# Trainium2: two transformer blocks on one core, with the products at stage boundaries ordered by row block and some operands produced turned

## What is computed

```python
for i in range(4):                      # first block; kinds A, B, C, A
    q, k, v, ... = split(x @ w_in)      # 12 heads of 64, rotary on the first 16 columns
    mix = attention_of_kind(q, k, v)    # A: indexer picks 64 keys; B: dilated; C: causal here
    mk, mv = split(layer_norm(mem) @ w_mem_kv[i])
    mo = memory_attention(qm, mk, mv)   # 4 heads over 256 memory rows
    x = layer_norm(ALPHA * x + concat(mix, mo) @ w_out[i], ln1)
    x = layer_norm(ALPHA * x + (silu(g) * u) @ w_down, ln2)   # g, u = split(x @ w_gate_up)
for layer in range(2):                  # second block
    h = rms_norm(x, norm_g) * (1 + scale) + shift   # shift, scale, gate from c @ w_ada
    rq, rk, rv, rg, sq, sk, sv, sg = split(h @ w_in_2)         # 8 parts of 512 columns
    y = concat(retention(rq, rk, rv) * silu(rg), stick_breaking(sq, sk, sv) * silu(sg))
    x = x + gate * (y @ w_out_2)
return rms_norm(x, final_g)
```

## Time and profile before

| | |
|---|---|
| median of 3 runs | 1818.16 us (1815.0 to 1821.46) |
| the profiled execution's own time | 1820.88 us |
| its span in the profile | 1819.0 us |
| PE busy / DVE busy / ACT busy | 1670.5 us (92%) / 1090.0 (60%) / 743.6 (41%) |
| mean granted clock of PE | 0.955 |
| moved over DMA | 296.32 MB, mean 163 GB/s |

### The profile page before, as it was taken

The page is one execution under the profiler, slowest core; times in us unless marked ns, Lnnn a source line. Parts: engine busy times, 40 slices in busy tenths (PEclk is TensorE's granted clock), DMA queues, the critical chain, the costliest instruction groups (busy, mean ns, idle before and its releaser), DMA issues.

```text
span 1819.0 us, 19290 instructions
## 1 busy us (share of the span) xinstructions
PE 1670.5 (92%) x7900; PEld 1348.3 (74%) x7900; DVE 1090.0 (60%) x1470; ACT 743.6 (41%) x879; POOL 45.7 (3%) x74
## 2 busy tenths in 40 slices
PE   6888899999988999998899999888999979899987
PEld 5666778878767888786688878666788858776866
DVE  4854566557566566664666557836555667456634
ACT  4434344334433334344343333443343434654372
POOL 1000000000000000000000000000000000000000
PEclk8998899999999999999899999979999989998999
DMA  8341266655324565551266555313456535233421
GB/s 299 135 139 47 93 223 221 227 200 217 116 79 153 210 242 219 208 185 47 94 230 231 208 208 208 127 59 119 168 209 236 214 110 183 107 114 126 170 88 46
DMA packets 43111, 296.32 MB, mean 163 GB/s; under 512 B 4996, under 2 KB 5124, under 8 KB 8976
## 3 DMA queue, kind: packets, MB, share of 16 engines
q1 hardware_dynamic: 38592, 279.99, 42.1%
q0 software_dynamic: 4000, 14.00, 2.4%
q10 hardware_dynamic: 432, 1.11, 0.2%
HBM read 294.03 MB, written 1.05 MB: 162 GB/s over the span
## 4 chain that ended last, share of the span: by engine, by line
PE 79%; DVE 11%; ACT 6%; issue 2%; DMA 1%; POOLq 0%; SPq 0%; DVEq 0%; ACTq 0%; POOL 0%
PE psum L605 22%; PE psum L607 22%; PE psum L606 22%; DVE w_low L1077 3%; PE psum L628 2%; PE psum L787 2%; ACT w_high L898 2%; PE psum L665 2%; ACT work L971 1%; PE psum L799 1%; PE psum L769 1%; DVE neg_max L1333 1%; PE psum L718 1%; DMA w_raw<-in_weights 1%; PE psum L860 1%
## 5 line engine op out<-in xcount | busy, mean ns | idle before, releaser
L1077 DVE TENSOR_TENSOR w_low<-w_raw,w_high 128x2048 fp32r<-128x2048 f32 x242 | 552.1, 2290 | 378.8 <-ACT w_high L898 378.5
L605 PE MATMUL psum<-w_high,xt_high 128*128 128x512 f32 (+1 forms) x1536 | 618.5, 403 | 16.6 <-DVE w_low L1077 8.6
L607 PE MATMUL psum<-w_high,xt_low 128*128 128x512 f32 (+1 forms) x1536 | 606.1, 395 | 0.0
L606 PE MATMUL psum<-w_low,xt_high 128*128 128x512 f32 (+1 forms) x1536 | 605.3, 394 | 0.0
L898 ACT ACTIVATE w_high<-w_raw 128x2048 fp32r<-128x2048 f32 x242 | 459.9, 1911 | 254.6 <-PE psum L607 248.7
L605 PEld LDWEIGHTS psum<-w_high,xt_high 128*128 128x128 f32 x1536 | 296.4, 193 | 80.6 <-issue 13.6
L607 PEld LDWEIGHTS psum<-w_high,xt_low 128*128 128x128 f32 x1536 | 295.3, 192 | 62.7
L606 PEld LDWEIGHTS psum<-w_low,xt_high 128*128 128x128 f32 x1536 | 296.4, 193 | 57.1
L605 PE MATMUL psum<-w_high,ht_high 128*128 128x512 f32 x352 | 138.2, 393 | 6.3 <-DVE ht_low L1383 6.3
L607 PE MATMUL psum<-w_high,ht_low 128*128 128x512 f32 x352 | 137.8, 391 | 0.0
L606 PE MATMUL psum<-w_low,ht_high 128*128 128x512 f32 x352 | 137.7, 391 | 0.0
(11 more groups left out here) (201 smaller groups left out, 1382.0 us busy)
## 6 DMA issues: line engine op xcount, KB each, us to landing
w_raw<-in_weights SPq DMA_DIRECT2D x266, 1024.0 KB, 4.8
norm_params<-in_ln_g POOLq DMA_DIRECT2D x8, 512.0 KB, 4.0
norm_params<-in_ln_b POOLq DMA_DIRECT2D x8, 512.0 KB, 5.3
x_rows<-in_x SPq DMA_DIRECT2D x2, 512.0 KB, 4.6
arena<-in_mem POOLq DMA_DIRECT2D x2, 512.0 KB, 19.7
norm_params<-in_norm_g POOLq DMA_DIRECT2D x2, 512.0 KB, 3.8
out_rows<-x_rows ACTq DMA_DIRECT2D x2, 512.0 KB, 2.6
mem_kv<-in_decay POOLq DMA_DIRECT2D x1, 768.0 KB, 4.8
```

The costliest lines, as they stand in the source:

```text
L605: e.matmul(dst, a_hi, b_hi, start=first, stop=False)
L606: e.matmul(dst, a_hi, b_lo, start=False, stop=False)
L607: return e.matmul(dst, a_lo, b_hi, start=False, stop=last)
L1077: e.tensor_tensor(K.w_lo[:, s, :], K.w_raw[:, r, :], K.w_hi[:, s, :].bitcast(F32), ALU.subtract).then_inc(K.taken.hit(t), 1)
```

## The change

- **Split in two.** `high` and `low` of a tile are steps of their own. After each product step the list has: `low` of the tile rounded last, then `high` of the next if a ring slot is free (`split`). The rings hold five tiles. One background step follows every product step instead of every second.
- **Order at boundaries.** `group` holds all tiles of two blocks (4), multiplies all of them for row block 0 and then all for row block 1. It is used for `w_out`, the first two up steps, the first projections, 7 and 3, and `w_out_2`; the last four down steps are ordered likewise. Sum, norm, rms and modulation of a row block follow its own last product, and the transposes of row block 0 stand among the products of row block 1 (and the other way round).
- **Turned operands.** For sq, sk, memory keys and memory queries the operands change places, so that the product comes out turned: 576 matmuls of 512 columns become 1152 of 256 columns, and 64 transposes of 128 x 128 go (16 + 16 + 32).
- **Memory products** of all four layers are made in layer 0 beside the indexer; those of layers 1 to 3 are put in DRAM (3 transfers out on POOL's queue) and fetched when needed (3 in). They no longer stand at ln2.
- **Feed-forward:** silu and product double buffered, `ht` fourfold; down lags by three steps; one ada tile in each of the steps 3 to 8.
- **Second block:** projections 0 and 1, then sq and sk turned, then 6 and 2 beside stick breaking, then 7 and 3 beside retention, then `w_out_2`.
- Small: one set of norm parameters; sums of ada tiles go through the ring of turning banks; the narrow tile is loaded only as far as it is used (576 columns).

```diff
-RING = 3
+RING = 5
...
+    def split(self):
+        self.low()
+        if self.owed:
+            self.owed -= 1
+            self.high()
+        self.owed, self.given_back = self.owed + self.given_back, 0
...
+    def on(self):
+        self.split()
+        self.step_background()
...
+    def block(self, name, layer, cols, gen, then, what="half"):
+        uses = [self.gemms.take() for _ in range(RB)]
+        for half in range(2):
+            t = self.tile(name, layer, cols, what, 4 * half)
+            for rb in range(RB):
+                self.gemm(t, rb, half, gen, "gemm", uses[rb])
+                if half:
+                    then(rb, uses[rb], t)
+                self.on()
...
+    def group(self, blocks, gen, after):
+        t = [[self.tile(name, layer, cols, what, 4 * half) for name, layer, cols, what, _ in blocks]
+             for half in range(2)]
         for rb in range(RB):
+            uses = [self.gemms.take() for _ in blocks]
+            for half in range(2):
+                for n, (*_, then) in enumerate(blocks):
+                    self.gemm(t[half][n], rb, half, gen, "gemm", uses[n])
+                    if half:
+                        then(rb, uses[n], t[half][n])
+                    after[rb][len(blocks) * half + n]()
...
-    def residual_norm(self, key, left, fill, gen):
...
+    def norm(self, key, rb):
+        self.add("stats", (key, rb))
+        self.add("gain", (key, rb))
+        self.add("bias", (key, rb))
...
+        def rest():
+            self.on()
             self.drain()
+            self.xt(mix, 1)
+            self.norm(key, 0)
...
+        def turned():
+            self.xt(("ff", layer), 0)
+            self.split()
+        self.group([("w_out", layer, h * BLK, "half", sums(h)) for h in range(2)], mix,
+                   [[self.on, self.on, self.on, rest], [self.split, self.split, turned, self.split]])
...
+                    if j.kind in BOTH:
+                        for n in range(2):
+                            dst, c = psum[:, bank, n * SEQ:n * SEQ + SEQ], at + rb * SEQ
+                            cols = slice(c + n * P, c + n * P + P) if turned else slice(c, c + SEQ)
+                            rows = slice(None) if turned else slice(n * P, n * P + P)
...
+                            m = products(e, dst, *both, first and n == 0, last and n == 1)
```

More of the change, by code:

```diff
@@ L361, in load_norm, with feed_forward, gate, then @@
         self.add("load_norm", key)
-    def residual_norm(self, key, left, fill, gen):
[L366 to L385, removed]
-        acc = [self.wide.take() for _ in range(RB)]
[L388 to L391, removed]
+    def norm(self, key, rb):
+        self.add("stats", (key, rb))
+        self.add("gain", (key, rb))
+        self.add("bias", (key, rb))
+    def feed_forward(self, layer):
+        gen, out = ("ff", layer), ("ln2", layer)
+        acc = [self.wide.take() for _ in range(RB)]
+        def gate(step):
+            def then(rb, use, tile):
+                self.up_use[layer, step, rb] = use
+                self.add("gate", Ff(layer, step, rb, use, tile))
+            return then
         def turn(step):
@@ L409, in feed_forward @@
                 self.add("load_gain", 0)
[L410 to L422, removed]
+                self.beside(self.modulation(0, range(4)))
@@ new lines, in first_layer @@
+        if layer == 0:
+            self.beside(self.memory_norm())
+            self.block(w_in, at, 3 * MIX, gen, qi[-1])
+            project(0)
+            narrow()
+            self.drain()
+            self.beside(self.indexer_work(layer))
+            self.memory()
+        else:
+            self.group([qi if kind == "A" else proj(0), proj(0) if kind == "A" else proj(1)], gen,
+                       [[self.split, self.split, late, queries], [self.on] * 4])
+            if kind == "A":
+                narrow()
+                self.beside(self.indexer_work(layer))
@@ L472, in late, with out_and_forward, sums, then @@
+    def out_and_forward(self, layer):
+        mix = ("mix", layer)
+        key = ("ln1", layer)
+        def sums(h):
+            def then(rb, use, tile):
+                self.add("residual", Residual(key, rb, h, tile, "gemm", use, True))
+                if h and rb:
+                    self.norm(key, rb)
+            return then
+        def rest():
+            self.on()
             self.drain()
+            assert self.units[layer, 1][-1].kind == "mem"
             self.xt(mix, 1)
-        key = ("ln1", layer)
@@ L576, in make, with turned @@
+        def turned():
+            if layer + 1 < DEPTH_2:
+                self.xt(("sin", layer + 1), 0)
+            else:
+                self.add("final", 0)
+            self.split()
+        self.group([("w_out_2", layer, h * BLK, "half", sums(h)) for h in range(2)], mix,
+                   [[self.split, self.split, lambda: self.xt(mix, 1), self.split],
+                    [self.split, self.split, turned, self.split]])
     def make(self):
```

883 lines of the change are left out of this document (505 added, 378 removed).

## The result

The changed kernel takes **1768.41 us** (median of 4 runs, 1766.37 to 1769.45), the one before 1817.26 in the runs beside it. The ratio is 0.973, 95% interval 0.971 to 0.975: faster by 49 us, where 123 were forecast, and 8 us above the top of the range. The sign was right, the size was not. The profiled execution's span is 1767.0 us, so the sum can be checked against it.

A forecast was written before the change was run, and what follows sets the result against it. PE was taken as the bound: 1558 us of need plus 137 lost (start 32, attention 42, feed-forward 6, ln2 1.5, before second block 7, second block 36, clock 12) gave 1695 us; range 1650 to 1760.

The forecast's parts named there:

- Turned operands: Products with operands swapped: 1152 of 256 columns at 0.120 us each, cost +7.7 us; 64 dropped transposes save 7.
- Norm beside products: Attention, `w_out`, ln1: two products cover 5.4 us of the 4.9 us norm chain; four stretches lose 42 us instead of 152.
- Start: First 90 us: second `low` stands behind the memory rows' gain; no gain, 32 us lost, as before.
- Second block: Waits at rotary, stick breaking, retention and layer boundary, final norm and store: 36 us lost instead of 54.
- Clock: Whole kernel: half clock follows waits of some us, few left outside the start; 12 us lost.
- rival (a): Attention stretches and second block: short gaps remain and the clock does not recover, +53 us, 1748 us; chance 0.14.
- the indexer's surplus: Layer 3's attention stretch: 17 us more lost than layer 1, put down to indexer DVE work; two thirds taken to stay.
- The fifth slot at nothing: Ring of rounded tiles: the fifth slot counted as covered, so priced at nothing.
- (b): Rival, turned products: half-width products cost 0.215 us each, giving 1804 us; chance 0.04.
- (d): Rival, norms: waits only move, each norm waiting for sums in the new order; about 1818 us, no change; chance 0.03.
- (c): Rival, weight loads: weights come too late through three load buffers, some +58 us, 1753 us; chance 0.06 for this milder form.
- (c)'s slower form: Weight loads: a full ring holds `high` and the load buffers for 21.8 us, 1830 us, slower than before; chance 0.04.

The follow-up runs named there:

- the run on the start: Norm of the memory rows begun three product steps later, against the changed kernel (1768.41 us): 1767.2 us.
- The run says 25 us: In a group, the low of an already rounded tile put ahead of row block 1's sum and norm, against the changed kernel (1768.41 us): 1743.05 us.
- the run gives 19: Second block's three rotary steps put one after the other, a product step apart, against the changed kernel (1768.41 us): 1749.05 us.
- the run with both edits: Rotary steps one after the other and low ahead of row block 1's sum and norm, together, against the changed kernel (1768.41 us): 1723.31 us.

## Why the prediction was wrong

**Right.** *Turned operands*: 0.120 us taken, 0.12 measured (the cost works out at +7.5 us, not +7.7); at the price of 0.112 or of 0.215 the sum would have been 9 lower or 109 higher. The Trainium skill's rule for an isolated matmul ("TensorE: Matmul & The Clock Gate", section "Back-to-back issue gap") makes it 109 ns, an estimate; the trace has a tenth more. *Norm beside products*: the wait of 4.70 is gone, layer 0's attention loses 12 us, 11 forecast, and undoing the order at one place costs 17. *Start*: no gain, as said; it lost 39 instead of 32, which the run on the start did not explain. Some 4 us of what it lost more than before (39 against 31) are clock: (1 - clock) x busy is 8.6 us there, 4.2 before.

**Wrong, and by how much.** The sum lost 137, the trace 215. Three steps carry most of it; they overlap, since the clock of step 3 is in what the runs give for steps 1 and 2:

1. *At ln1 "1.5 to 2 [...], where a `low` stands behind the norm", under attention, `w_out` and ln1.* I had seen the low behind the norm and priced it by the norm it waits for, not by what waits for the low. Three lows stand there, and PE waits 2.6 us in each layer, in the first up steps, and 4.3 at the boundary of the second block's layers. The run says 25 us with the clock; the forecast held some 6 to 8 of it.
2. *Second block, "three of them and two lows stand before the turned products: 6".* The place was right. The wait is 7.4 us a layer, and its half clock comes on top: the run gives 19 for two layers, the forecast had 12.
3. *Clock, "few are left outside the start: 12".* It is 49, of which 39 lie outside the start. This is the largest single error, 27 us. I took half clock to follow waits of 5 us, from one place in the trace; here waits of 1.5 to 4.3 us are often followed by it too. Steps 1 and 2 bring 22 of the 49 with them, as the run with both edits shows (27 are left), so this is not a separate cause, but a factor that I should have put on every wait left standing. The rival (a) had the mechanism, small gaps that keep the clock down, but as a rest that stays whatever is done; where the edits took waits away, it went with them.

With the two order errors taken out the kernel runs in 1723, and the forecast is 28 us below that. Counted by stretch in that run, the second block is then where it was forecast (35 lost against 36). Layer 3 is 16 over (32 lost against 16; I took a third of the indexer's surplus to be hidden, and nothing shows that it is), layer 1 8, the start 7, the boundary before the second block 5, layer 2 4 to 5; the 12 set apart for the clock are in these.

*The fifth slot at nothing.* "Covered" was wrong in the plain sense: without it the change is worth nothing (1818.65). My sum assumed the ring never to be short, so the number did not suffer; but the reader was told that the slot was an aside, and the gain hangs on it.

*Rivals.* (b) fell to the profile. (d) fell as a whole (1768, not 1818), but steps 1 and 2 are waits that moved. (c): `w_high`'s wait for loads is there (197 us), as I said it would be for (c). It is not what held PE back: the two edits took 45 us away with the same loads and buffers, and behind all of PE's waits for `w_low` but the first, `w_high` was ready. A fourth buffer takes ACT's wait away (6.6) for no gain; that was run with four slots only. As a sign, ACT's wait was badly chosen: a wait of an engine that is ahead shows only what it waits for, not that anyone waits for it. The price of (c)'s slower form does not follow from its own formula: 266 x 21.8 / 3 is 1933, not 1830.

## What to carry to other kernels

Where one engine prepares operands in a fixed order, price a reordering by the last operand it pushes back and by the idle time just ahead of it: a ready low may stand behind a norm that has still to wait. Count some half clock on every wait that stays, not on the long ones alone. Try the depth of the ring as well as the number of load buffers, one at a time, and look at whether PE's wait moves, not ACT's: then see whether the operand that PE waits for was itself waiting for its input, or ready and standing behind other work.

## What the runs showed of the hardware

- Filling a wait of 2.6 us on PE with transposes of 128 x 128 kept the granted clock at 1.00, where it fell to 0.71 in the four us behind it without them; with the other places filled as well the kernel is 9 us faster. The Trainium skill ("TensorE: Matmul & The Clock Gate", section "A second HAM failure mode: psum-queue depth-cycling") says that frequent short idle times of PE between groups of matmuls make the clock swing; the runs agree, and add that work without use in the gap stops it there.
- Not every short wait is followed by half clock. In the changed kernel the same wait, at the same place of the four layers, was followed by it three times (0.71 from 237 to 241, 0.58 from 864 to 868, 0.57 from 1222 to 1226); the fourth time, in layer 1, the granted clock from 551 to 555 was 1.00:

```profile
550.79 0.50 PE L772 MATMUL psum<-w_high,xt_high 128*128 128x512 f32 x1 [2.60 <-DVE w_low L1266]
551.12 0.39 PE L773 MATMUL psum<-w_low,xt_high 128*128 128x512 f32 x1
551.36 0.40 PE L774 MATMUL psum<-w_high,xt_low 128*128 128x512 f32 x1
```

- Half-width products of the rounded kind start 0.12 us apart, just over half of 0.227, with a new operand loaded for each: behind 1048 of the 1152 the next start came within 0.13 us.
